# A hybrid decoder step: x loaded turned in the index stage, row factors applied behind the projections

## The reference, cut to what matters

```python
def _rms_norm(x, gain):
    y = xf * lax.rsqrt(jnp.mean(xf * xf, axis=-1, keepdims=True) + EPS)
    return (y * gain.astype(jnp.float32)).astype(x.dtype)
# xn = _rms_norm(x, att_norm)
q, k, v, iq, ik, iw, gate = _split(xn @ w_in, ATT_SIZES)
ik = _rms_norm(ik, ik_gain)
iw = iw * (IDX_HEADS ** -0.5 * IDX_DIM ** -0.5)
# indexer: score[t, l] = sum_h iw[t, h] * relu(iq[t, h] . ik[l])
# then the 256 best l of every t, and softmax attention over these alone
```

## Time and profile before

| | us |
|---|---|
| median of 3 runs | 1866.98 |
| lowest and highest run | 1861.58, 1869.72 |
| profiled execution, span (its own time is given only as this span) | 1911.6 |
| TensorE busy | 1733.9 (91%) |
| VectorE busy | 1274.5 (67%) |
| ScalarE busy | 759.6 (40%) |
| POOL busy | 518.8 (27%) |

### The profile page before, as it was taken

One profiled execution on the slowest core, in us unless ns is written; L12 is line 12 of the kernel. 1 busy time (PEld: TensorE's weight loads), 2 busy tenths in 40 slices (PEclk: granted clock), 3 DMA queues, 4 the chain that ended last, 5 costly groups with the idle time before them and its releaser, 6 DMA issues. The chain is left out here.

```text
span 1911.6 us, 26707 instructions
## 1 busy us (share of the span) xinstructions
PE 1733.9 (91%) x10053; PEld 994.6 (52%) x10053; DVE 1274.5 (67%) x2068; ACT 759.6 (40%) x1805; POOL 518.8 (27%) x588
## 2 busy tenths in 40 slices
PE   6888999999989999999989769989996878999997
PEld 5453444444445566664434334434434776777774
DVE  1389957899976799964885334535553576777671
ACT  3447778852224344322212222222211544655550
POOL 2121300100101111002117666767522502222320
PEclk9999999999999999999999979999998899999999
DMA  4125530110124112003215445445579445343220
GB/s 132 36 91 174 180 135 14 44 39 28 56 111 176 66 67 101 32 12 136 67 44 145 123 122 154 147 143 157 149 266 325 119 130 141 109 105 87 76 63 36
DMA packets 159447, 207.37 MB, mean 108 GB/s; under 512 B 45160, under 2 KB 109120, under 8 KB 159296
## 3 DMA queue, kind: packets, MB, share of 16 engines
q1 hardware_dynamic: 117336, 149.65, 23.7%
q0 software_dynamic: 16896, 50.35, 8.7%
q10 hardware_dynamic: 25088, 5.66, 1.5%
HBM read 161.89 MB, written 43.74 MB: 108 GB/s over the span
## 5 line engine op out<-in xcount | busy, mean ns | idle before, releaser
L930 PE MATMUL acc<-w_qg,xnT 128*128 128x512 f32 x384 | 169.1, 593 | 0.0
L2130 POOL DMA_INDIRECT home<-in_cache_v,rowidx x128 | 129.6, 1013 | 68.7 <-issue 35.7
L1147 DVE MAX8 top_v<-scores 128x8 f32<-128x4100 f32 x32 | 141.6, 4426 | 0.3
L1149 DVE FIND_INDEX8 top_i<-top_v,scores 128x8 uint32<-128x4100 f32 x32 | 141.5, 4423 | 0.0
L1151 DVE MATCH_REPLACE8 scores<-top_v,scores 128x4100 f32<-128x4100 f32 x32 | 141.2, 4413 | 0.0
L3450 PE MATMUL PY<-home,ogT_dn 128*128 128x512 f32 x288 | 133.6, 609 | 5.8 <-DVE y_t L3936 5.1
L1348 PE MATMUL ring<-w_out_att,ogT_blk 128*128 128x512 f32 x256 | 111.4, 593 | 2.8 <-DMA w_out_att<-in_att_w_out 1.7
L930 PEld LDWEIGHTS acc<-w_qg,xnT 128*128 128x128 f32 x384 | 71.1, 190 | 81.6 <-issue 81.5
L930 PE MATMUL acc<-w_kvq,xnT 128*128 128x512 f32 x256 | 111.4, 593 | 0.0
L2453 DVE SCALAR_TENSOR_TENSOR y_ch<-x_pad,conv_w,y_ch 128x1024 f32<-128x1024 f32 x72 | 92.5, 1285 | 2.6
L186 ACT ACTIVATE junk_topk_h<-key_mask,bs_cand 128x640 f32<-128x640 f32 (+1 forms) x88 | 86.1, 981 | 15.7 <-DVE bs_cand L196 10.8
(11 more groups left out here) (535 smaller groups left out, 3586.0 us busy)
## 6 DMA issues: line engine op xcount, KB each, us to landing
S_s<-in_dn_w_in SPq DMA_DIRECT2D x24, 512.0 KB
qkv_d<-y_ch SPq DMA_DIRECT2D x24, 512.0 KB
qkv_t<-qkv_d SPq DMA_DIRECT2D x8, 1536.0 KB, 8.1
home<-in_dn_w_in SPq DMA_DIRECT2D x5, 2048.0 KB, 11.2
x<-in_x_all SPq DMA_DIRECT2D x9, 512.0 KB, 3.7
out_y_all<-y_t SPq DMA_DIRECT2D x9, 512.0 KB, 2.9
w_kvq<-in_att_w_in SPq DMA_DIRECT2D x2, 2048.0 KB, 7.8
w_qg<-in_att_w_in SPq DMA_DIRECT2D x2, 2048.0 KB, 12.6
```

The source lines that it names most:

```text
L930: ins = pe.matmul(acc[rows(n), k % ACC, :], xnT[:, kk, cols(n)], w[:, kk, :], start=(kk == 0), stop=(kk == KT - 1))
L1147: link(dve.max(v, scores[:]))
L1149: dve.max_index(top_i[:, 8 * r:8 * r + 8], v, scores[:])
L2130: pool.indirect_dma_start(vg[:, j % VR, c, :], None, cv, bass.IndirectOffsetOnAxis(ap=rowidx[:, c, query(j):query(j) + 1], axis=0)).then_i ...
```

## The change

x is given in a second layout, x_cols (features by rows), and is loaded straight into xnT. VectorE multiplies it in place by the gains, one a partition (`gains`, 8 instructions a trio). The 72 transposes of x, their copies and the row norms are gone. ScalarE still squares x in natural layout, but behind the keys and among the query copies. The index queries stay without their row factor and the head weights take its square; the key's norm takes the factor's effect through the epsilon. Factors go to DRAM (rs_d), come back as one row on all partitions (rs_row), and POOL multiplies them into xnT in eight instructions in the sample stage, one behind every third gather. Key buffers go from 2 to 3. TensorE's order is new (keys 0 and 1, queries 0, keys 2 to 5, queries 1, keys 6 to 8, first scores, queries 2, last scores). POOL's first eight gathers stand in front of the last three tiles' factors. The search steps are 13 in the index stage, all between the two groups of scores, and 31 in the sample stage.

```diff
-TOPK_IN = {"index": (0, 4), "index_late": (4, 15), "sample_scores": (15, 44), "heads": (34 + 32, len(SEARCH))}
+TOPK_IN = {"index": (0, 13), "sample_scores": (13, 44), "heads": (34 + 32, len(SEARCH))}
...
+            sp.dma_start(xnT[:, 0:4, trio(0)], xv[:, 0:4, trio(0)]).then_inc(xt_in[0], 16)
+            sp.dma_start(gxc[:], d["att_norm_cols"]).then_inc(gxc_in, 16)
+            sp.dma_start(wk[:], wv[:, :, IK0:G0]).then_inc(wk_in, 16)
+            sp.dma_start(xnT[:, 4:8, trio(0)], xv[:, 4:8, trio(0)]).then_inc(xt_in[1], 16)
+            sp.dma_start(wq[:, :, 0:256], wv[:, :, IQ0:IQ0 + 256]).then_inc(wq_in[0], 16)
+            sp.dma_start(wq[:, :, 256:512], wv[:, :, IQ0 + 256:IK0]).then_inc(wq_in[1], 16)
+            for n in range(XR):
+                load(n)
...
+            sp.dma_start(xnT[:, :, trio(1)], xv[:, :, trio(1)]).then_inc(xt_in[2], 16)
...
+            sp.dma_start(causal[:], d["c_causal"]).then_inc(causal_in, 16)
+            for n in range(XR, 2 * XR):
+                load(n)
+            sp.dma_start(xnT[:, :, trio(2)], xv[:, :, trio(2)]).then_inc(xt_in[3], 16)
+            sp.wait_ge(rsi_ok, 1)
+            with nc.allow_non_contiguous_dma(reason="64 x 8 head weights"):
+                for b in range(DB):
+                    sp.dma_start(d["iwl_d"][b].rearrange("h t -> t h"), iw_nat[b * DS:(b + 1) * DS, 0, :]).then_inc(iwl_out, 16)
+            store(0)
+            store(1)
+            with nc.allow_non_contiguous_dma(reason="64 x 8 head weights"):
+                sp.wait_ge(iwl_out, 16 * DB)
+                for r in range(2):
+                    sp.dma_start(iwcol[r * 64:(r + 1) * 64, :], d["iwl_d"].rearrange("b h t -> (h t) b")).then_inc(iwl_in, 16)
+            store(2)
+            for n in range(2 * XR, NT):
+                load(n)
+            for n in range(3, 6):
+                store(n)
+            sp.wait_ge(rsx_ok, NT)
+            with nc.allow_non_contiguous_dma(reason="one factor per row"):
+                sp.dma_start(d["rs_d"][:, 0:NS].rearrange("o p -> p o"), rsx[0:NS, 0, :]).then_inc(rs_out, 16)
+                sp.dma_start(d["rs_d"][:, NS:].rearrange("o (n p) -> p (o n)", p=P), rsx[:, 1:NT, :].rearrange("p n o -> p (n o)")).then_inc(rs_out, 16)
+            for n in range(6, NT):
+                store(n)
...
             def rms_x(n):
                 pool.wait_ge(ssx_ok, n + 1)
+                link(pool.tensor_scalar(msx[:, n, :], ssx[:, n, :], 1.0 / DM, EPS, ALU.mult, ALU.add))
+                pool.tensor_scalar(epsm[:, n, :], msx[:, n, :], EPS, None, ALU.mult)
+                link(pool.tensor_tensor(rsx[:, n, :], msx[:, n, :], mhalf[:], ALU.pow))
+                link(pool.tensor_tensor(rs2[:, n, :], rsx[:, n, :], rsx[:, n, :], ALU.mult))
+                pool.tensor_scalar(rs2[:, n, :], rs2[:, n, :], IH ** -0.5 * ID ** -0.5, None, ALU.mult).then_inc(rsx_ok, 1)
             def rms_ik(n):
+                q = rows(n)
                 pool.wait_ge(ssi_ok, n + 1)
+                pool.wait_ge(rsx_ok, n + 1)
+                pool.tensor_scalar(iw_nat[q, n, :], ikr[q, n % 3, ID:ID + IH], rs2[q, n, :], None, ALU.mult)
+                link(pool.tensor_scalar(msi[q, n, :], ssi[q, n, :], 1.0 / ID, None, ALU.mult))
+                link(pool.tensor_tensor(msi[q, n, :], msi[q, n, :], epsm[q, n, :], ALU.add))
+                pool.tensor_tensor(rsi[q, n, :], msi[q, n, :], mhalf[q, :], ALU.pow).then_inc(rsi_ok, 1)
             for n in range(3):
                 rms_x(n)
+                rms_ik(n)
             pool.memset(wred[:], 0.0).then_inc(zeroed, 1)
+            for n in range(3, 6):
+                rms_x(n)
+                rms_ik(n)
             pool.wait_ge(idx_ok, 1)
             gather_keys(pool, d, keep, k_in, 0, RING)
+            for n in range(6, NT):
+                rms_x(n)
+                rms_ik(n)
...
+            keys(0)
+            keys(1)
+            queries(0)
+            for n in range(2, 6):
+                keys(n)
+            for n in range(3):
+                transpose_ik(n)
+            pe.wait_ge(ptf_ok, 1)
+            pe.matmul(kq[:, 2, 0:DB * NGI], e16[:], ptf[:], start=True, stop=True).then_inc(ptb_ok, 1)
+            queries(1)
+            for n in range(6, NT):
+                keys(n)
+            for n in range(3, 6):
+                transpose_ik(n)
+            pe.wait_ge(idx_ok, 1)
+            pe.wait_ge(iq_ok, 8)
+            pe.wait_ge(tp_evac, 6)
+            for i in EARLY:
+                key_scores(i)
+            queries(2)
+            for n in range(6, NT):
+                transpose_ik(n)
+            pe.wait_ge(iq_ok, 12)
+            pe.wait_ge(tp_evac, NT)
+            pe.wait_ge(zeroed, 1)
+            for i in LATE:
+                key_scores(i)
...
+            take_keys(0)
+            take_keys(1)
+            for g in range(4):
+                take_queries(0, g)
+                if g < 3:
+                    square_x(g)
+            for n in range(2, 6):
+                take_keys(n)
             for n in range(3):
+                evac_ik(n)
+            for g in range(4):
+                if g < 3:
+                    square_x(g + 3)
+                take_queries(1, g)
+            for n in range(6, NT):
                 square_x(n)
+                take_keys(n)
+            for n in range(3, 6):
+                evac_ik(n)
+            for i in EARLY:
+                relus(i)
+            for g in range(4):
+                take_queries(2, g)
+            for n in range(6, NT):
+                evac_ik(n)
+            for i in LATE:
+                relus(i)
...
-            def norm_x(n):
-                dve.wait_ge(rsx_ok, n + 1)
-                dve.scalar_tensor_tensor(x[:, n % XR, :], x[:, n % XR, :], rsx[:, n % 2, :], gx[:], ALU.mult, ALU.mult).then_inc(xn_ok, 1)
+            def gains(r):
+                if r == 0:
+                    dve.wait_ge(gxc_in, 16)
+                for k in range(KT):
+                    if r == 0 and k % 4 == 0:
+                        dve.wait_ge(xt_in[k // 4], 16)
+                    elif k == 0:
+                        dve.wait_ge(xt_in[r + 1], 16)
+                    dve.tensor_scalar(xnT[:, k, trio(r)], xnT[:, k, trio(r)], gxc[:, k:k + 1], None, ALU.mult).then_inc(xg_ok, 1)
...
+            gains(0)
+            gains(1)
             dve.wait_ge(pt_in, 64)
             dve.tensor_copy(ptf[:], pti[:]).then_inc(ptf_ok, 1)
+            dve.wait_ge(gik_in, 16)
+            for n in range(3):
+                norm_ik(n)
             dve.wait_ge(causal_in, 16)
             for i in range(FREE):
                 if i > 0:
                     dve.memset(key_mask[:, KM[i]:KM[i] + i * P], 0.0)
                 dve.tensor_copy(key_mask[:, KM[i] + i * P:KM[i + 1]], causal[:])
+            dve.wait_ge(ptb_ok, 1)
+            link(dve.tensor_scalar(idxf[:], kq[:, 2, 0:DB * NGI], float(RPG), j8[:], ALU.mult, ALU.add))
+            dve.tensor_copy(idx[:].rearrange("p a b -> p (a b)"), idxf[:]).then_inc(idx_ok, 1)
+            gains(2)
...
+            ins.then_inc(prep_ok, 1)
+            for n in range(3, NT):
+                norm_ik(n)
+            for i in EARLY:
+                add_parts(i)
+            topk(*TOPK_IN["index"])
+            for i in LATE:
+                add_parts(i)
...
+            sp.wait_ge(env["stores"]["rs_out"], 32)
+            sp.dma_start(keep["rs_row"][:], d["rs_d"].partition_broadcast(P)).then_inc(rs_in, 16)
...
                 gather_keys(pool, d, keep, k_in, n, n + 1)
+                if n % 3 == 2:
+                    k = (n - RING) // 3
+                    if k == 0:
+                        pool.wait_ge(rs_in, 16)
+                    pool.tensor_tensor(xnT[:, k, :], xnT[:, k, :], keep["rs_row"][:], ALU.mult)
...
-    ins["att_norm_rows"] = np.ascontiguousarray(np.broadcast_to(a["att_norm"].reshape(1, DM), (P, DM)))
+    ins["x_cols"] = np.ascontiguousarray(np.concatenate([x_all[0:NS], x_all[P:]], 0).T)
+    ins["att_norm_cols"] = np.ascontiguousarray(a["att_norm"].reshape(KT, P).T)
```

265 lines of the change are left out of this document (73 added, 192 removed).

## The result

The changed kernel takes 1872.82 us in the median of 7 runs (1870.89 to 1875.29), the kernel before 1864.05 in 7 runs beside it: ratio 1.0045, 95% interval 1.0032 to 1.0057, or 8.8 us more. The prediction said 1859.6 with a range to 1868: wrong in sign, and outside its range. The profiled execution has a span of 1871.3 us.

A forecast was written before the change was run, and what follows sets the result against it. TensorE and VectorE were taken to alternate in the index stage, so time saved there counts at the end. Index stage -16.7 and sample stage +9.3 gave -7.4 us: 1859.6 us as a median, range 1849 to 1868.

The forecast's parts named there:

- Index stage: Front of the kernel: without transposes and norms of x, the last group of adds begins 16.7 us sooner.
- Both rms of a tile are now nine instructions, about 2.9 us: Index stage, POOL: time per tile for its factors, which puts the first add at 76.4 us.
- Sample stage: Stage after the index stage: POOL's eight products and VectorE's added work lengthen it by 9.3 us.
- Its own two ends: Sample stage: VectorE ends at about 100.4 us and TensorE at 100.6 after its start, against 92 now.
- TensorE came 4.2 us late, not 8.6: Sample stage: products delay POOL's gathers, moving TensorE's end by 4.6 + 2 + 2 = 8.6 us.
- the two more steps: Sample stage, VectorE: 31 search steps instead of 29, costing 3.4 us.
- the constant: Sample stage, VectorE: it starts perhaps 2 us later behind the broadcast of the factor row.
- on average 1.7 in short steps and 0.7 in the long ones: 8.6: Sample stage: average time each POOL product holds VectorE, by length of search step, 8.6 us in sum.
- 3 x 1.7 + 5 x 0.7: Sample stage: three products fall beside short search steps and five beside long ones, giving 8.6 us of holds.
- only the last instruction of a step can be held: Sample stage: POOL's product holds just the two-operand instruction of 0.16 us ending each search step; counts stay free.
- The third rival: Sample stage: VectorE loses all eight products in full, 20.8 us, and ends it; total +3.8, 1870.8 us; chance 0.08.
- I am wrong if ... a later stage changes its length: Stages behind the sample stage: stated sign of failure; head_project was to be entered with the same work in both versions.

The follow-up runs named there:

- pair_72_more: Changed kernel with 72 tiny transposes added on TensorE in the index stage, where it waits; 1926.95 us, ratio 1.0007 to the kernel before.
- pair_after: The changed kernel again, unedited, on the same chip and in the same rounds as the one with 72 transposes more; 1930.15 us, ratio 1.0034 to the kernel before.
- the control: Changed kernel with 72 tiny transposes behind the last product of the whole kernel; 1877.4 us, ratio 1.0083 to the kernel before.

## Why the prediction was wrong

**Index stage**: -16.7 predicted, -13.5 in the pair of profiles, -17.9 between the means of all. This term held. The order of events held: queries at 14.7 (13.5 said), gathers done at 68.1 (67.1), adds released by POOL's last factor. "Both rms of a tile are now nine instructions, about 2.9 us" was short: 3.57 from tile to tile. Hence 79.1 for the first add (76.4) and 122.8 for the second group (119.5).

**Sample stage**: +9.3 predicted, +16.9 measured. This is the step that failed first. (Its own two ends, 100.4 and 100.6 against 92, give 8.4 to 8.6; nothing in it gives the 0.7 above that.) TensorE came 4.2 us late, not 8.6: the gathers landed in a median of 5.3 us, where 6.5 was taken, and the waits for them were 7.5 us in sum. VectorE was put level with TensorE, at 100.4; it ended at 108.9. Of its terms the two more steps (3.4) held, the constant came 2.9 us late and not 2, and "on average 1.7 in short steps and 0.7 in the long ones: 8.6" measured 16.8, and 15.5 to 17.4 in eight profiles with whole products behind gathers.

Two things in that term were wrong. First, its count: "3 x 1.7 + 5 x 0.7" puts three products beside short steps. The late constant, the two more steps and the holds themselves kept VectorE in its short steps until 201.6, 50 us after the stage's start, where the kernel before left them after 31, so six products fell there: 3.0 us more. Second, their size: the six held 2.56 us each, not 1.7, another 5.2. The average took it that the two engines meet at random. But a compare held to a product's end (167.25) is followed by the next but one 3.3 us later (170.53, after two steps), and POOL's three gathers take 3.66 (167.22 to 170.88). So that compare begins 0.35 us before the next product, in the last part of its gather, and loses the product in full. In all eight profiles the second and third product of a burst found it there while the steps were short, 0.3 to 0.6 us ahead. The two products beside long steps held 0 and 1.4 us, near the 0.7 forecast. That only the last instruction of a step can be held was wrong too (L135 in front of it is held as well), but it matters little for the sum: the two stand 0.2 us apart.

The Trainium skill, SBUF — State Buffer, section "Who interferes with whom", had what I left out: a tensor_scalar that does not write its accumulator out can take the shared pair of ports as well. L135 is such a one. The counting passes L118 do write it: 54 of them ran beside a product in ten profiles and none was longer by more than 0.01 us, such as the 1.08 and 1.22 us beside the product at 214.74. The trace agrees with both statements. The prediction cited the part on the accumulator and drew from it that the last instruction alone is held.

The third rival had the right engine and nearly the right size (VectorE ending the stage at 112.6 after its start, against 108.9), for a partly wrong reason: it had the counting passes held. It got 0.08. That its total is so near (1870.8 against 1872.8) is luck: it has nothing for the last stage.

**What lay outside the sum**: "I am wrong if ... a later stage changes its length". One did, and the sum had put the stages behind at nothing. The last stage takes 446 us instead of 439 in the profiles. -13.5 + 16.9 + 6.8 is 10.2, against 8.8 measured, for this one pair; in the means of all profiles the first two stages cancel (-17.9 and +17.9), and the last stage's 6 us stand against the 8.8.

The runs show that the places of the long gaps follow the places of TensorE's instructions: padding moved them, and every gap ends just behind a load. That the places set the stage's length is shown only in the mean (441.3 against 447.5): single profiles of the two kinds overlap (pair_72_more 445.9, pair_after 442.9). How much of the median it carries is settled only to between 3 us (side by side, not clear of the noise) and 7 (against the control, less its own 2.2). The larger part of the difference is time at the lower level of the clock; why there is more of it with the shifted places, in most executions but not all, was not settled.

## What to carry to other kernels

Before a two-operand product goes on POOL, list what VectorE runs beside it, the smallest instructions too: with a chain of short dependent steps there, count the products nearly in full (15.5 to 17.4 us lost to eight of 2.5) and do not rely on splitting. A factor per row belongs where another engine already reads the data: as the scale of a copy out of PSUM it cost 0.1 us a copy on an engine with idle time and saved the 17. And a change of instruction counts early on shifts the loads of all later code: compare the stages that were not touched, put the counts back before judging, and take several profiles of each, since one stage alone differed by 9 us between executions.

## What the runs showed of the hardware

A compare of 128x2 elements, 0.17 us alone, was held up to 3.1 us by one product, 7.9 us by three in a row, and 3.6 us by eight short ones. A scalar_tensor_tensor of the same size on integers was held 3.15. Between pieces of 0.44 us VectorE got in only sometimes. Counting passes, which write their accumulator out, were never held.

In the last stage, from 90 us into it on, every gap of TensorE with no wait of its own and over 0.6 us (112 of them, up to 3.9 us) ended 2.2 to 3.0 us after the start of an instruction load. The 144 records fewer, 1400 us earlier, moved these gaps; with them back the medians were 3 to 7 us lower, the lower figure inside the noise.

The best version found (factor in ScalarE's copies, POOL's factors ahead of the gathers, 72 instructions of padding) took 1843.84 us against 1861.52 of the kernel before.
